# The gate factor of an expert layer's diagonal, moved from ScalarE to GpSimd

## The reference, cut to what matters

```python
def one_block(args):
    xt, et, gt = args                      # 128 tokens, their 128 expert numbers and 128 gates
    u = expert_u[et]
    v = expert_v[et]
    act = jax.nn.gelu(jnp.einsum('tnd,td->tn', u, xt)) * gt
    return jnp.einsum('tn,tnd->td', act, v)
```

## Time and profile before

| | us |
|---|---|
| median of three runs | 1628.71 |
| lowest and highest | 1627.07, 1630.46 |
| the profiled execution | 1626.22 |
| its span in the trace | 1624.4 |
| row loop, first transfer issued to last matmul | about 333 to 1028 |
| busy in the span: PE, DVE, ACT, POOL | 1201.1, 932.0, 421.6, 339.8 |

### The profile page before, as it was taken

One profiled execution on the slowest core, in us unless ns is written; L12 is line 12 of the kernel. 1 busy time (PEld: TensorE's weight loads), 2 busy tenths in 40 slices (PEclk: granted clock), 3 DMA queues, 4 the chain that ended last, 5 costly groups with the idle time before them and its releaser, 6 DMA issues.

```text
span 1624.4 us, 26294 instructions
## 1 busy us (share of the span) xinstructions
PE 1201.1 (74%) x11106; PEld 819.1 (50%) x11106; DVE 932.0 (57%) x2059; ACT 421.6 (26%) x1060; POOL 339.8 (21%) x315
## 2 busy tenths in 40 slices
PE   7989888963484433447747766579987877999997
PEld 6468773850152100115514442257887853888843
DVE  2977664555986888795677656221445343455501
ACT  3011400012432322453363332223242300111100
POOL 1000011114453344444546453000000000000000
PEclk9998998985597555569868887699999999999999
DMA  9552388799999999999999999424200023344441
GB/s 371 187 182 90 106 290 293 243 363 336 421 415 343 407 421 415 417 414 418 419 418 420 420 419 419 152 78 156 104 9 4 4 106 104 117 154 149 150 148 73
DMA packets 112295, 412.34 MB, mean 254 GB/s; under 512 B 10648, under 2 KB 35744, under 8 KB 78896
## 3 DMA queue, kind: packets, MB, share of 16 engines
q0 software_dynamic: 44576, 297.35, 45.2%
q1 hardware_dynamic: 63360, 106.48, 19.2%
q10 hardware_dynamic: 4240, 6.83, 1.9%
HBM read 408.51 MB, written 2.12 MB: 253 GB/s over the span
## 4 chain that ended last, share of the span: by engine, by line
PE 52%; DMA 26%; DVE 10%; ACT 6%; issue 3%; POOL 2%; ACTq 0%; POOLq 0%; DVEq 0%
PE psum L500 25%; DMA arena<-in_experts,arena 24%; PE psum L510 7%; PE psum L1691 5%; PE psum L2175 5%; DVE arena L1270 3%; PE psum L1301 3%; POOL arena L1257 2%; PE psum L596 1%; ACT arena L1281 1%; PE psum L2059 1%; PE psum L719 1%; ACT arena L1286 1%; DMA arena<-in_lora_up 1%; DMA weights<-in_w_att_out 1%
## 5 line engine op out<-in xcount | busy, mean ns | idle before, releaser
L1301 PE MATMUL psum<-arena 128*32 128x512 f32 x1024 | 194.5, 846 | 295.8 <-ACT arena L1286 292.5
L500 PE MATMUL psum<-actT,weights 128*128 128x256 f32 x1824 | 401.3, 382 | 5.2 <-ACT actT L613 2.3
L1257 POOL DMA_INDIRECT arena<-in_experts,arena x256 | 309.9, 1211 | 402.1 <-PE psum L1301 324.4
L500 PEld LDWEIGHTS psum<-actT,weights 128*128 128x128 f32 x1824 | 348.7, 192 | 56.9 <-ACT actT L613 5.6
L1301 PEld LDWEIGHTS psum<-arena 128*32 128x32 f32 x1024 | 23.8, 126 | 401.8 <-ACT arena L1286 373.9
L1270 DVE CUSTOM_DVE_ANT_0 arena<-arena 128x1024 f32<-128x1024 f32 x96 | 116.8, 1223 | 58.7 <-DMA arena<-in_experts,arena 57.9
L1270 DVE CUSTOM_DVE_ANT_0 arena<-weights,arena 128x1024 f32<-128x1024 f32 x96 | 117.2, 1224 | 54.6 <-DMA arena<-in_experts,arena 52.8
L1276 ACT ACTIVATE arena<-arena 128x2 f32<-128x2 f32 x128 | 26.0, 203 | 401.4 <-DVE arena L1270 401.3
L1270 DVE CUSTOM_DVE_ANT_0 arena<-normed,arena 128x1024 f32<-128x1024 f32 x64 | 77.3, 1226 | 37.6 <-DMA arena<-in_experts,arena 36.7
L1691 PE MATMUL psum<-arena 64*64 64x64 f32 (+1 forms) x2816 | 82.3, 227 | 15.0 <-DVE arena L1808 7.1
L1691 PEld LDWEIGHTS psum<-arena 64*64 64x64 f32 x2816 | 78.5, 139 | 23.0 <-issue 11.5
(11 more groups left out here) (354 smaller groups left out, 1607.8 us busy)
## 6 DMA issues: line engine op xcount, KB each, us to landing
weights<-in_w_in SPq DMA_DIRECT2D x18, 2048.0 KB, 8.6
arena<-in_ada_wT POOLq DMA_DIRECT2D x48, 512.0 KB, 6.0
weights<-in_ffn_w_up SPq DMA_DIRECT2D x22, 1024.0 KB, 6.5
weights<-in_ffn_w_down SPq DMA_DIRECT2D x5, 2048.0 KB, 7.7
weights<-in_w_out SPq DMA_DIRECT2D x4, 2048.0 KB, 12.9
weights<-in_w_peer_q SPq DMA_DIRECT2D x4, 2048.0 KB, 10.6
arena<-in_experts,arena POOLq DMA_INDIRECT x256, 13.5
weights<-in_w_ple_gate SPq DMA_DIRECT2D x2, 2048.0 KB, 10.4
```

Source lines behind the costliest of these rows:

```text
L500: mm = nc.tensor.matmul(out[:, c * T:(c + 1) * T], w[:, k, c * P:(c + 1) * P], act[:, k, :], start=(k == 0), stop=(k == kc - 1))
L1257: nc.gpsimd.indirect_dma_start(out=rows[:, n % RING, :], out_offset=None, in_=dram["experts"], in_offset=bass.IndirectOffsetOnAxis(ap=eidx ...
L1301: mm = nc.tensor.matmul(SUMS[sum_part(k, i), i, :], diag[:, pos, :], rows[:, pos, D + 512 * i:D + 512 * (i + 1)], start=first, stop=last, ...
```

## The change

POOL now writes gate times `ident_q` into the row's slot of `diag` (`pool_gated`, one 128x32 `tensor_scalar` a row), four rows behind the transfer that it has just issued: after issuing row n it does this for row n - 4. Ahead of the first of each 32 rows it waits for `gates_done`. The new semaphore `gated_ok` counts these. ACT loses the 128x1 products (`acts` and its semaphore) and its own waits for `gates_done`; it scales the slot in place by the gelu instead of scaling `ident_q`, once `gated_ok` says that the slot is written. The order of the two factors changes, no other work does.

```diff
@@ -1242,6 +1242,17 @@
+        def pool_gated(pool, n):
+            b, i = divmod(n, NSEL)
+            if i % (NSEL // QUARTERS) == 0:
+                pool.wait_ge(S("gates_done"), QUARTERS * b + i // (NSEL // QUARTERS) + 1)
+            nc.gpsimd.tensor_scalar(diag[:, n % RING, :], K("ident_q"), gate[:, b, i:i + 1], None, ALU.mult).then_inc(
+                S("gated_ok"), 1)
+
+        BEHIND = RING // 2
@@ -1258,6 +1269,10 @@
                 ).then_inc(S(f"row{n % RING}"), 16)
+                if n >= BEHIND:
+                    pool_gated(pool, n - BEHIND)
+            for n in range(TB * NSEL - BEHIND, TB * NSEL):
+                pool_gated(pool, n)
@@ -1274,17 +1289,12 @@
             nc.scalar.activation(gelu[:, g, 0:count], dots[:, g, 0:count], ACT.Gelu_apprx_tanh).then_inc(S("gelu_ok"), 1)
-            if isinstance(t, int):
-                act.wait_ge(S("gates_done"), QUARTERS * b + (t * RING + g * GROUP + count - 1) // (NSEL // QUARTERS) + 1)
             act.wait_ge(S("gelu_ok"), t * PER_TURN + (GROUPS * b + g + 1))
-            for j in range(count):
-                nc.scalar.activation(acts[:, g, j:j + 1], gelu[:, g, j:j + 1], ACT.Copy,
-                                     scale=gate[:, b, bass.ds(t * RING + (g * GROUP + j), 1)]).then_inc(S("acts_ok"), 1)
             for k, pos, n, filled in turn_slots(b, t, g * GROUP, count):
                 j = k - g * GROUP
-                act.wait_ge(S("acts_ok"), rows_ahead(b, t, g) + j + 1)
-                nc.scalar.activation(diag[:, pos, :], K("ident_q"), ACT.Copy,
-                                     scale=acts[:, g, j:j + 1]).then_inc(S("diag_ok"), 1)
+                act.wait_ge(S("gated_ok"), rows_ahead(b, t, g) + j + 1)
+                nc.scalar.activation(diag[:, pos, :], diag[:, pos, :], ACT.Copy,
+                                     scale=gelu[:, g, j:j + 1]).then_inc(S("diag_ok"), 1)
```

More of the change, by code:

```diff
@@ L313, in build @@
         gate = r.take(TB * NSEL).rearrange("p (b n) -> p b n", b=TB)
-        dots, gelu, acts = [r.take(RING).rearrange("p (g n) -> p g n", n=GROUP) for _ in range(3)]
+        dots, gelu = [r.take(RING).rearrange("p (g n) -> p g n", n=GROUP) for _ in range(2)]
         diag = r.take(RING * QP).rearrange("p (g n) -> p g n", g=RING)
@@ L1314, in groups_of_rows @@
                     end = min(last // PER_TURN, TURNS - 1)
-                    if group is act_group:
-                        eng.wait_ge(S("gates_done"), TB * QUARTERS)
                     with eng.Fori(t, end) as i:
```

## The result

The changed kernel takes 1639.21 us in the median (1634.56 to 1640.74), beside 1630.46 us (1627.07 to 1635.39) for the kernel before in the same comparison: a ratio of 1.0057, 95% interval 1.003 to 1.0084. A fifth execution of the changed kernel, in a slow state of the chip, took 3077.31 us and is in neither the range nor the ratio. The kernel is slower by some 9 us where 4 us less were forecast. The profiled execution took 1638.92 us, its span is 1637.1 us.

The account below looks back on a forecast made before the run. DMA was taken to bound the row loop; -4.3 (ACT's queue) - 0.8 (two pairs) + 1.0 (DVE and POOL in each other's way) = -4.1 us, from 1628.7 to 1624.6. The range ran from 1621 to 1638.

Parts of the forecast that it names:

- What bounds the loop: Row loop: DMA is full at 417 to 418 GB/s, so one row takes 2.57 us.
- POOL then needs 1.5 + 0.5 = 2.0 us a row: Row loop: issue 1.2 plus gap 0.31, and product 0.5, stay hidden under the 2.57 us that DMA allows.
- the upper bound of 1.4: POOL's product in the row loop: costs 0 to 1.4 us, including a wait for DVE and a gap; 0.5 taken.
- Rival 3: Row loop: POOL becomes the bound, about 1710 us, or 1639 if only DVE's densest stretches suffer; chance 0.12.
- 0.85 us more: POOL's product in the row loop: may wait for DVE as a transfer's issue does, 0.85 us more.
- The start of the loop: Around the first nine rows: `lora_up` lands sooner, ACT issues `ctx` earlier, first matmul and ninth row follow; -4.3 us.
- The reload: Between POOL's fifth row issue and first product: an ISA row reloads POOL's library, taken as 12.0 us.
- R = 351.4: Loop start: R is the end of the library reload, 339.4 + 12.0, inside the window of full gain (about 350 to 359).
- rival 1: Loop start: library reload quick or done while POOL waits, `lora_up` lands as before; 1628.9 us, no change; chance 0.27.
- The two pairs: First and last pair of the loop: ACT's diagonal starts 0.39 us earlier in each, together -0.8 us.
- DVE held by POOL: Row loop: DVE may wait for POOL's read; 0 to 2 us, 1.0 taken, including a pair's late second transfer.
- ACT's wait: Row loop: ACT waits for POOL's product; four rows cost at least 6.9 us against DMA's 10.3, so nothing is late.

Follow-up runs that it names:

- e1: The changed kernel with POOL only writing the constant 1 into the slot, reading nothing; 0.9988 of the kernel before.
- e9: The kernel before plus a POOL product of one column instead of 32 after each transfer, into an unused spare buffer; 1.0058 of the kernel before.
- e7: The changed kernel with all eight first transfers ahead of the first four products; 1.0046 of the kernel before.
- e6: The kernel before with ACT's load of `ctx` moved behind a few pairs of rows (fourth piece of beside work); 0.9997 of the kernel before.
- e11: The kernel before with ACT's load of `ctx` moved right behind the fourth pair of rows; 1.0012 of the kernel before.
- e3: The kernel before without ACT's 128x1 products and nothing new on POOL, the gate left out of the result; 0.9987 of the kernel before.
- e5: The changed kernel with one 128x128 `tensor_tensor` for four rows behind every fourth transfer, first behind the eighth; 0.9994 of the kernel before.
- e14: The changed kernel with four one-row `tensor_scalar` products in a row behind every fourth transfer, first behind the eighth; 1.0017 of the kernel before.
- e13: The changed kernel with the same product a row at the same place, written as a `tensor_tensor`; 1.0008 of the kernel before.
- e2: The kernel before, ACT untouched, plus POOL's full product after each transfer into a spare buffer nobody uses; 1.0036 of the kernel before.

## Why the prediction was wrong

**What bounds the loop: right.** DMA is full at about 417 GB/s and a row costs 2.57 us; every kernel with 412 or more in both windows is within 0.2% of before.

**The step that failed: "POOL then needs 1.5 + 0.5 = 2.0 us a row of the 2.57 that DMA allows. It stays hidden."** Two things were wrong in it. The size: the product takes 0.908 us, not 0.5 with its gap; the value chosen lay near ACT's row of the same shape and gave being held little weight, though the 1.79 us issue was at hand and the upper bound of 1.4 had been worked out from it. A whole row costs POOL 2.31 us, not 2.0. And the form of the argument: it compared means. 2.31 us a row is still below 2.57; the loss comes from stretches in which POOL's row costs more than that, 2.62 us from 655 to 740 and 3.11 from 840.16 to 868.12, with single rows of 3.7, and the 4.4 us that a transfer had stood in the queue are soon used up by that. The transfers' own cost had been read rightly (1.2, measured 1.199), and the gaps of a row are 0.20 us, less than the 0.31 that was added.

**Rival 3 is what happened**, with its price: "if only the stretches in which DVE is densest suffer, some 10 us: 1639". It had 0.12. That the time is met to the microsecond is luck: the "some 10 us" is worked out from nothing, and DVE isn't at its densest where the loss arises (80% busy from 655 to 740 and 77% from 840 to 900 before, 87% from 540 to 655); its instructions are at their longest there. Against the rival were put POOL's 324 us of waiting and DVE's waits for rows, "half of the time". The latter is a misreading: 147.4 us are 22% of the loop; only the number of waits, 120, is near half of the rows. And both are sums over the loop. Nor would a look at POOL's waits by stretch have done: before the change it waited for PE 42.2 us from 655 to 740, 1.2 us a row of 35, as in the rest of the loop (324.4 / 256 = 1.27). What differs there is the price of what POOL runs, and that hangs on DVE's instructions beside it. POOL's own transfers give half a warning: they were dearer from 840 to 900 already, 34.54 / 24 = 1.44 us each against 54.03 / 46 = 1.17 from 540 to 655, but not from 655 to 740, 38.30 / 35 = 1.09. The share of DVE's long instructions, above, marks both. What is held is the instruction that reads: at the same place it took 142 ns in the mean when it only wrote the slot (e1), and 750 when it read one column (e9). That a product may wait for a second DVE instruction that follows the first without a gap, and that this hangs on its form, the prediction didn't foresee: "0.85 us more" as the upper bound of a hold was too small, the longest being 3.36 - 0.35 = 3.0.

**The start of the loop: -4.3 forecast, about -0.3 measured.** The reload was assumed to last until R = 351.4, 12.0 us, which was an estimate from other loads; no run shows such a time. The timeline of the changed kernel shows it nowhere as a wait (idle before and its releaser in brackets):

```profile
340.82 0.94 POOL L1268 DMA_INDIRECT arena<-in_experts,arena  x1 [0.30 <-issue]
...
349.75 2.46 POOL L1251 TENSOR_SCALAR arena<-const,arena 128x32 f32<-128x32 f32 x1 [7.98 <-DVE arena L1241]
...
353.19 0.42 ACTq L536 DMA_DIRECT2D arena<-in_lora_up  x1
...
364.47 2.15 ACTq L536 DMA_DIRECT2D arena<-in_ctx  x1
```

The first product begins at 349.75, 0.11 us behind the end of the gates' copy, so the reload lay within the 8 us in which POOL waited anyway, as rival 1 had it. e7 leaves at most 4.3 us for it, where the prediction took 12.0. The first product took 2.46 us beside DVE, in e7 as in the changed kernel. `lora_up` landed 364.47 - 353.19 = 11.3 us after its issue instead of 12.0. The ninth transfer went out 371.07 - 335.7 = 35.4 us after the first, 36.1 before: 0.7 us of gain, of which the forecast gave 0.4 to the shorter step of ACT's first pair. That is rival 1's case and not the forecast's. And e6 and e11 show a second flaw under the first: even six us at that place are worth at most 1.2 in the loop. The prediction took it that a ninth transfer issued earlier ends the hole as much earlier; its time to landing grew by 2.3 and 2.8 us instead, and `ctx`, which had loaded about the end of the hole, took DMA time from the rows (1 MB, 2.5 us at the 419 GB/s of that stretch in e6). Why the transfers were slow there stays open.

**The two pairs, -0.8: not contradicted.** e3 gives -1.3 us of loop and 0.9987 (0.9971 to 1.0003), which can't be told from nothing.

**DVE held by POOL, 0 to 2 us: right, and harmless.** L1285 takes 1230 to 1233 ns in the mean in its three groups, 1223 to 1226 before, 256 x 7 ns = 1.8 us in all, while DVE still waits 136.4 us for rows. The 1.0 that the sum carried for this "and the late second transfer" is the term that should have held the 7 us.

**ACT's wait: 27.3 us, hidden,** as said. ACT's busy time came to 376.3 us, not 360: a part of L1281's 61 us had run beside other instructions of ACT, and the scaling in place takes 314 ns instead of 305.

## What to carry to other kernels

An engine with slack on the average can still be the bound: put its price per row against the rate stretch by stretch, held time included, not over the loop. GpSimd's small product cost here what DVE's work beside it made it cost (0.35 us clear, 0.91 in the mean). What helped was fewer of them (e5, 0.61 us for four rows), several in a row (e14, 2.45 for four), a form that only wrote (e1, 0.14) or a `tensor_tensor` in place of the `tensor_scalar` (e13, 0.49). DVE's busy share didn't tell here where that is; the length of its instructions did, and how often one followed another without a gap. Before counting an idle stretch of DMA as a gain, test whether a transfer issued earlier lands earlier.

## What the runs showed of the hardware

- The product of the changed kernel (`POOL L1251 TENSOR_SCALAR arena<-const,arena 128x32`) took 0.353 us at the least, 0.386 in the mean of the 30 beside which DVE was idle, 0.908 in the mean of all and 3.357 at the most. The 135 of over 0.6 us all overlapped with a dot product (L1285) or another DVE instruction with two inputs, and the 14 that met only DVE's searches took 0.384 to 0.396; 40 of 251 outlasted two DVE instructions, 37 of them where the second followed the first without a gap. The same product as `tensor_tensor` (e13) took 0.234 at the least, 0.490 in the mean and 1.373 at the most, and none of 251 did.
- One column instead of 32 (product unused in both) cost the loop as much (e9 681.4, e2 680.9 us, before 675.4); a write of the whole slot took 0.142 us in the mean and left the loop at 676.7 (e1).
- The issue of an indirect DMA varied beside DVE as well: 0.94 us in the median before and 1.00 in the changed kernel, up to 1.99 and 2.05, with a mean of 1.2 in both.
- The instruction ahead of GpSimd's first `tensor_scalar` (`MODIFY_POOL_CONFIG`, two records of 43 ns in e7) kept POOL from it for at most 4.3 us, with DMA at 426 GB/s.
- A row transfer issued at 365 us (e6, e11), six us earlier in the loop than before, took 13.7 and 14.2 us to land instead of 11.4, with DMA at 60 GB/s for 8 us of e6 meanwhile; no run shows why.
